# One of three weight sums made by an adding transfer that GpSimd issues, and VectorE's list in another order

## What is computed

```python
def swiglu(x, w_gate, w_up, w_down):
    return (jax.nn.silu(x @ w_gate) * (x @ w_up)) @ w_down
```

## Time and profile before

| What | us |
|---|---|
| median of 3 runs | 1737.55 |
| lowest and highest | 1736.27, 1737.61 |
| the profiled execution's own time | 1736.21 |
| its span | 1734.4 |
| PE busy | 1720.8 (99%) |
| VectorE busy | 1206.8 (70%) |
| ScalarE busy | 876.1 (51%) |
| GpSimd busy | 783.0 (45%) |

### The profile page before, as it was taken

The page is one execution under the profiler, slowest core; times in us unless marked ns, Lnnn a source line. Parts: engine busy times, 40 slices in busy tenths (PEclk is TensorE's granted clock), DMA queues, the critical chain, the costliest instruction groups (busy, mean ns, idle before and its releaser), DMA issues.

```text
span 1734.4 us, 27783 instructions
## 1 busy us (share of the span) xinstructions
PE 1720.8 (99%) x9696; PEld 1454.7 (84%) x9696; DVE 1206.8 (70%) x1809; ACT 876.1 (51%) x1486; POOL 783.0 (45%) x423
## 2 busy tenths in 40 slices
PE   9999999999999999999999999999999999999998
PEld 7899988888888777788888999988866889999887
DVE  6898984278867885236469899843785598998532
ACT  6455552266554477785344555522425445555222
POOL 2344354467565433325453344544533534435443
PEclk9999999999999999999999999999999999999999
DMA  5333333322333221112323333332361323333222
GB/s 178 98 108 102 104 104 96 127 93 88 110 110 113 64 72 50 50 49 86 97 92 95 104 109 104 103 97 97 104 146 61 97 85 107 103 106 109 97 98 73
DMA packets 50518, 168.54 MB, mean 97 GB/s; under 512 B 6264, under 2 KB 7032, under 8 KB 50304
## 3 DMA queue, kind: packets, MB, share of 16 engines
q1 hardware_dynamic: 47088, 161.34, 29.9%
q10 hardware_dynamic: 3344, 6.05, 1.3%
HBM read 161.84 MB, written 2.11 MB: 95 GB/s over the span
## 4 chain that ended last, share of the span: by engine, by line
PE 92%; DVE 4%; issue 2%; ACT 1%; POOL 1%; DMA 0%; POOLq 0%; SPq 0%; ACTq 0%; DVEq 0%
PE bank L620 16%; PE bank L622 16%; PE bank L621 16%; PE bank L746 8%; PE bank L914 7%; PE bank L732 6%; PE bank L734 5%; PE bank L735 5%; PE bank L744 3%; PE bank L959 2%; PE bank L985 2%; PE bank L1087 1%; PE bank L976 1%; PE bank L749 1%; DVE input_low L1691 1%
## 5 line engine op out<-in xcount | busy, mean ns | idle before, releaser
L487 POOL TENSOR_TENSOR weights_low<-raw_weights,weights_high 128x1024 fp32r<-128x1024 f32 x192 | 470.1, 2453 | 558.4 <-ACT weights_high L1204 530.5
L1204 ACT CAST weights_high<-raw_weights 128x1024 fp32r<-128x1024 f32 x244 | 254.1, 1045 | 296.9 <-DMA raw_weights<-weights 278.0
L528 POOL TENSOR_TENSOR weights_low<-raw_weights,weights_high 128x512 fp32r<-128x512 f32 x100 | 149.6, 1518 | 286.4 <-DVE weights_low L1849 286.4
L620 PE MATMUL bank<-input_high,weights_high 128*128 128x512 f32 x624 | 246.2, 395 | 2.4 <-DVE input_low L1691 1.7
L621 PE MATMUL bank<-input_high,weights_low 128*128 128x512 f32 x624 | 243.1, 390 | 0.0
L622 PE MATMUL bank<-input_low,weights_high 128*128 128x512 f32 x624 | 243.1, 390 | 0.0
L732 PE MATMUL bank<-input_mixed,weights_high 128*128 128x256 f32 x600 | 171.9, 287 | 0.0
L735 PE MATMUL bank<-input_mixed,weights_high 128*128 128x256 f32 x600 | 169.2, 282 | 0.0
L746 PE MATMUL bank<-input_mixed,weight_sum_high 128*128 128x512 f32 x400 | 148.9, 395 | 0.0
L620 PEld LDWEIGHTS bank<-input_high,weights_high 128*128 128x128 f32 x624 | 117.2, 188 | 30.7 <-issue 5.0
L622 PEld LDWEIGHTS bank<-input_low,weights_high 128*128 128x128 f32 x624 | 117.1, 188 | 24.8
(11 more groups left out here) (330 smaller groups left out, 4340.3 us busy)
## 6 DMA issues: line engine op xcount, KB each, us to landing
raw_weights<-weights SPq DMA_DIRECT2D x294, 512.0 KB, 3.6
out_t<-out_t SPq DMA_DIRECT2D x8, 256.0 KB, 2.1
residual<-x_t SPq DMA_DIRECT2D x6, 256.0 KB, 5.9
glu_stacked<-glu_padded ACTq DMA_DIRECT2D x24, 64.0 KB, 4.6
glu_stacked<-glu_padded SPq DMA_DIRECT2D x24, 64.0 KB, 4.7
mem_in<-mem_t ACTq DMA_DIRECT2D x1, 1024.0 KB, 4.9
tile<-forget_sums ACTq DMA_DIRECT2D x4, 256.0 KB, 3.5
raw_weights<-weights SPq DMA_DIRECT2D x3, 256.0 KB, 5.8
```

Of the source, the lines that this page charges most:

```text
L487: pool.tensor_tensor(wl[:, u % RING, :], raw[:, u % RING, :], wh[:, u % RING, :].bitcast(F32), ALU.subtract).then_inc(low_done, 1)
L528: pool.tensor_tensor(wl[:, u % RING, w], raw[:, u % RING, w], wh[:, u % RING, w].bitcast(F32), ALU.subtract).then_inc(low_done, 1)
L620: pe.matmul(out, wh[:, u % RING, w], rh, start=start, stop=False)
L1204: act.copy(wh[:, u % RING, :], raw[:, u % RING, :]).then_inc(high_done, 1)
```

## The change

The third sum is no longer an operation of VectorE. GpSimd starts a transfer, `third_sum`, that reads U0 a second time from the chip's memory (128 rows of 2 KB, 256 KB) and adds it onto G0 in the raw slot. It waits for the first sum of that pair, since the first sum still reads G0, and stands in GpSimd's list behind `next_quarter`. The semaphore `third_sum` rises by 16 when it has landed, and ScalarE waits for that before it makes the high part.

The semaphore `sums` counts three in a pair now. ScalarE makes the high part of the third sum behind the copy of the next pair's first product, no longer ahead of it. VectorE's additions of products come directly behind each other, 1833 ahead of 1829, and the fourth sum behind line 1840.

```diff
+                def third_sum(q, i=None):
...
+                    u = u0 + 2 * (plain + q)
+                    source = (T["weights"][u, :, 0:S] if i is None else
+                              T["weights"][bass.ds(i * 4 + u, 1), :, 0:S].rearrange("a p n -> p (a n)"))
+                    pool.wait_ge(sem("sums"), pairs_before(name, 3) + at(3 * q + 1, 6))
+                    pool.dma_start(raw[:, (u + 1) % RING, 0:S], source, accum_op=ALU.add).then_inc(sem("third_sum"), 16)
+
                 for u in range(first, u0 + 2 * plain):
                     low_part(u)
                 next_quarter(0)
+                third_sum(0)
                 looped = mixed // 2 * 2 - 2
                 with pool.Fori(0, looped // 2) as i:
                     for c in range(2):
                         pair_low(c, i)
                         next_quarter(c + 1, i)
+                        third_sum(c + 1, i)
...
@@ ScalarE, frame
-                        sum_high(wh[:, gate, 0:S], raw[:, gate, 0:S], at(4 * p + 7, 4))
                         if p >= 0:
                             copy_product(copies[:, 1 - c, 0, :], bank[2 - b][:, 0:HALF], at(5 * p + 5, 5))
+                        act.wait_ge(sem("third_sum"), 16 * pairs_before(name, 1) + at(16 * p + 32, 16))
+                        act.copy(wh[:, gate, 0:S], raw[:, gate, 0:S]).then_inc(sem("sum_high"), 1)
+                        if p >= 0:
                             act.wait_ge(sem("products"), pairs_before(name, 5) + at(5 * p + 6, 5))
-                        sum_high(sum_h[2][:, :], sums[2 + (p + 1) % 2][:, :], at(4 * p + 8, 4))
+                        sum_high(sum_h[2][:, :], sums[2 + (p + 1) % 2][:, :], at(3 * p + 6, 3))
@@ VectorE, frame
-                    if more:
-                        dve.tensor_tensor(gate[:, 0:S], gate[:, 0:S], up[:, 0:S], ALU.add).then_inc(sem("sums"), 1)
```

More of the change, by code:

```diff
@@ L541, in next_quarter, with at @@
                                        ALU.subtract).then_inc(sem("quarter_low"), 1)
+                def third_sum(q, i=None):
+                    def at(n, step):
+                        return n if i is None else i * step + n
+                    u = u0 + 2 * (plain + q)
[3 more added lines that the diff above has]
+                    pool.dma_start(raw[:, (u + 1) % RING, 0:S], source, accum_op=ALU.add).then_inc(sem("third_sum"), 16)
                 for u in range(first, u0 + 2 * plain):
@@ L554, in gate_up_lows @@
                         next_quarter(q + 1)
+                        third_sum(q + 1)
             pool.wait_ge(sem("first_low"), len(FIRST) + DVE_LOWS - 2)
@@ L1336, in sum_high @@
                 def sum_high(dst, src, at):
-                    act.wait_ge(sem("sums"), pairs_before(name, 4) + at)
+                    act.wait_ge(sem("sums"), pairs_before(name, 3) + at)
                     act.copy(dst, src).then_inc(sem("sum_high"), 1)
@@ L1805, in sum_at, with formed_at @@
                         return at(pairs_before(name, 4) + n, 4)
+                    def formed_at(n):
+                        return at(pairs_before(name, 3) + 3 * p + 3 + n, 3)
                     c, b, u = p % 2, 2 * ((plain + p) % 2), u0 + 2 * (plain + p) + 2
@@ L1817, in frame @@
                         dve.tensor_tensor(sums[0][:, :], gate[:, 0:S], gate[:, S:2 * S], ALU.add).then_inc(sem("sums"), 1)
-                        dve.wait_ge(sem("sums"), sum_at(4 * p + 5))
+                        dve.wait_ge(sem("sums"), formed_at(1))
                         dve.tensor_tensor(sums[1][:, :], sums[0][:, :], up[:, 0:S], ALU.add).then_inc(sem("sums"), 1)
@@ L1834, in frame @@
                                           ).then_inc(sem("partial"), 1)
-                    if more:
-                        dve.wait_ge(sem("sums"), sum_at(4 * p + 6))
-                        dve.tensor_tensor(s4[:, :], sums[1][:, :], up[:, S:2 * S], ALU.add).then_inc(sem("sums"), 1)
+                        dve.wait_ge(sem("partial"), at(pairs_before(name, 3) + 3 * p + 1, 3))
+                        dve.tensor_tensor(up_out[:, 0:HALF], bank[4][:, HALF:S], up_out[:, 0:HALF], ALU.add)
                     if now:
@@ L1842, in frame @@
                     if more:
+                        dve.wait_ge(sem("sums"), formed_at(2))
+                        dve.tensor_tensor(s4[:, :], sums[1][:, :], up[:, S:2 * S], ALU.add).then_inc(sem("sums"), 1)
                         dve.wait_ge(sem("sum_high"), sum_at(4 * p + 6))
```

4 lines of the change are left out of this document (2 added, 2 removed).

## The result

| | us |
|---|---|
| before, median of 4 runs | 1737.41 (1736.27 to 1737.61) |
| after, median of 4 runs | 1775.21 (1774.47 to 1775.98) |
| ratio | 1.0222, 95% interval 1.0209 to 1.0234 |
| predicted | 1772, range 1733 to 1832 |

The changed kernel is 37.8 us slower; the spans of the profiled executions differ by 39.9 us (1734.4 and 1774.3), that of the changed kernel being the slowest of its four. The median of the kernel before is from one run more than in the table ahead of the prediction. GpSimd's 528 and 540 have kept theirs.

The account below looks back on a forecast made before the run. TensorE was taken as the bound everywhere. Ring excess of 40 us over 50 pairs, less 2.9 head start and 2.3 for the stall, gave +34.8 on 1736.2: 1771.0, by the median 1772 us, range 1733 to 1832.

Parts of the forecast that it names:

- D: Time from the adding transfer's issue by GpSimd to its landing, forecast at 4.5 us, bounds 2.1 to 9.8.
- the ring: In each mixed pair, first sum through transfer, ScalarE, VectorE and GpSimd to the next first sum's end: D + 6.32 us.
- The second read: Part of D: the adding transfer must read its destination too, another 256 KB, 1.0 us, bounds 0 and 2.6.
- the load beside it: Part of D: the next up unit's load is under way when the transfer starts, 0.5 us, bounds 0 and 1.0.
- GpSimd's issue: Part of D: GpSimd makes up the list of what is moved, 0.4 us, bounds 0 and 1.30.
- The rival that the transfer is in time: D at most 3.7 us, nothing waits and the stall is gone: 1735 us by the median, chance 0.26.
- third rival: First sum gets ahead of GpSimd's low part, the ring is looser, free up to D = 4.6: 1735 us, chance 0.07.
- step 1: Start of the ring: the first sum ends, only then may the transfer start, issued by an idle GpSimd.
- limit of 3.7 us: Largest D at which the transfer is free, with the ring at D + 6.32 and a pair at 10.02 us.
- head start: Slack before TensorE feels GpSimd's late low parts, 0.97 us in each stage, 2.9 us for three, taken off the loss.
- the stall: TensorE's wait in the mixed pairs for VectorE's addition at line 1840, expected to go: 2.3 us, bounds 0 and 5.5.
- U1's product: Sign: with D over 3.7 us, TensorE idles ahead of line 746 or 744 for U1's low part from GpSimd's 528.

Follow-up runs that it names:

- order_early: Kernel before with VectorE's new order, no transfer, and GpSimd's low parts waiting only for the fourth sum: 1771.38 us, ratio 1.0201.
- order_only: Kernel before with only VectorE's list reordered (1833 ahead of 1829, fourth sum behind 1840), third sum still on VectorE: 1735.66 us, ratio 0.9991.

## Why the prediction was right, and where it was only lucky

The mechanism was right: a ring through the transfer, ScalarE, VectorE and GpSimd that is longer than TensorE's 10.02 us. The 1772 us came within 3 of the measured 1775, but that closeness is luck: D was put 0.3 us too high and the ring 0.1 us too low, which made the pairs too dear, and the ends of the stages, which cost 7.8 us, were put at nothing.

**The length of the transfer, step by step.** Predicted 4.5 us, measured 4.2 as the median. The second read was put at 1.0 us, and the experiment without it gives 3.2 against 4.2. The rest was put at 3.5 (2.6 for the plain rows, 0.5 for the load beside it, 0.4 for GpSimd's issue) and was 3.2. GpSimd's part was put at 0.4, and GpSimd is taken for 0.88 us by the adding transfer and 0.55 by the plain one. How much of that lies in D, and what the load beside it costs, no run took apart. The rule in the Trainium skill's "DMA: Bandwidth & Descriptors", 2.0 us plus the bytes at 436 GB/s, gives an estimated 2.6 us for the plain transfer; the measured median of 3.2 us is longer, though the shortest of the 50 took 2.6. The rival that the transfer is in time fell, since D was over 3.7. Its condition was also too wide: with 3.1 and 3.2 us two kernels still lost 5 us, one of them mostly at the ends of the stages.

**The ring.** Predicted D + 6.32, measured D + 6.25 in 32 turns and D + 7.0 in 15, on average D + 6.44 (the stages' first turns left out), but the pieces were not those of the prediction. It said that GpSimd's low part comes ahead of the first sum by 0.05 us however late both are. In those 32 turns the first sum is ahead by less than 0.1 us (156.48 against 156.49 in the turn shown), takes 0.69 us, and GpSimd's operation takes 1.85 us in place of 1.30. That is the premise of the third rival. Its conclusion was wrong, because the transfer stands behind GpSimd's low part in its list: what the first sum gains, the low part loses. In the form that was predicted, which the other 15 turns and most of those of the plain transfer show, the ring is D + 7.0, and nearly all of what is missing, 0.64 us, is the time from the end of the first sum to the issue, a term that step 1 put at nothing. With it the prediction's limit of 3.7 us would have been 3.0 to 3.1.

That operations of VectorE and GpSimd which both read two operands from the on-chip memory don't run side by side was in the rows (0.69 against 1.36 us) and held throughout: 0.68 against 1.78 us in order_early. The Trainium skill says in "SBUF — State Buffer", section "Who interferes with whom", that a VectorE instruction with two inputs from that memory contends with a GpSimd instruction that reads it, and that the order of issue decides who is held up; these rows agree. The prediction used it for one pair of operations only, and not for the ends of the stages.

**The sum.** Predicted for the pairs were 40 us, less a head start of 2.9, less 2.3 for the stall: 34.8. Measured are 30.6, 0.6 us a pair in place of 0.8. The 0.8 is off by D (4.5 against a mean of 4.18) and by the ring (6.32 against 6.44), which together make 0.6: 4.18 + 6.44 - 10.02. A head start isn't to be seen, since 50 times 0.6 is all that the pairs lost. Missing from the sum is what comes behind the stages: the prediction let their late finish cost nothing of its own, and 7.8 us came there, because VectorE's low parts of the hidden values now collide with GpSimd. The remaining 1.5 us are spread over the rest. The three stages aren't alike: the first transfer of g1 was the slowest of all (issued at 70.49, landed at 76.46), those of g2 and g3 with 3.7 and 3.9 us among the faster ones.

**The order.** 2.3 us predicted, 1.7 measured alone, with an interval that reaches nothing. In the changed kernel it can't be told.

**Where TensorE waits.** Predicted at U1's product for GpSimd's 528. It is there (line 760, 5.1 us), but more of it is two products later, where the next pair's first product waits for 540 (line 746, 10.8 us). Both stand behind the same wait of GpSimd. ScalarE's idle time ahead of the third sum's high part was named as a sign with 3 us or more in each pair; it was 2.3 us on average.

**What the change could have given.** VectorE's 34 us of third sums are worth nothing where it has slack, as predicted. They are worth much where it has none: with early low parts the kernel with VectorE's third sum took 1771 us and the one with the transfer 1737. The prediction had called VectorE's time worthless by itself; that holds for this order of the lists, not for a neighbouring one.

## What to carry to other kernels

When a step moves to a path that takes microseconds to answer, add up the ring that it closes, from the resource it needs back to itself, with the time from the semaphore to the issue, and compare it with the bound's period; then look whether every member of the ring has to be in it. Here one wait was wider than the data needed (GpSimd waited for the third sum's low part, where the fourth sum was enough), and taking that out gave all of the 38 us back. Look behind the last turn as well: engines that are late by unequal amounts can meet where they didn't before, which cost some 2.5 us a stage here.

Time of an engine that isn't the bound is still worth something as room for such a change, so try the two together before judging either.

## What the runs showed that I had not expected

- An adding transfer issued by GpSimd took 4.2 us for 256 KB, the same without adding 3.2 us, and half the size with adding 3.1 us. GpSimd itself is taken for 0.88 us by an adding transfer, whether of 256 or 128 KB, and for 0.55 us by a plain one.
- Where GpSimd is idle and waits for VectorE's first sum, the issue comes 0.64 us behind its end (154.32 to 154.96), where from VectorE's third sum to ScalarE it was 0.03 us. Where GpSimd comes from an operation of its own that ends later, the issue follows it at once (156.49 + 1.85 against 158.28).
- Two engines that collide can swap who goes first by a few hundredths of a microsecond, and the time from the first start to the last end stays the same (156.48 to 158.34, 152.49 to 154.32). Which of them pays decides which one's followers are late.
- Moving GpSimd's low parts ahead by some 2.6 us (from 6.65 to 4.09 us behind the start of the first sum), without any more work, made a kernel 36 us slower (order_early against order_only), only by what it ran beside.
